# Latent layer of a four-layer trunk: a ring of three transposed tiles, value products two steps behind, another order of projections, gates directly behind their unit

## The reference

```python
proj = h @ w_in                                  # c_q 256, c_kv 128, k_rope 64, g 2048
q = (rmsnorm(c_q, q_norm_g) @ w_uq)              # 16 heads x (128 + 64)
kv = (rmsnorm(c_kv, kv_norm_g) @ w_ukv)          # 16 heads x (128 keys + 128 values)
for i in range(S // 128):                        # 8 tiles of 128 queries
    s = q_nope @ k_nope.T + q_rope @ k_rope.T    # causal: keys 0 .. 128 (i + 1)
    p = softmax(s * scale)
    outs.append(p @ v)
return (o * silu(g)) @ w_out
```

## Time and profile before

| | us |
|---|---|
| median of three runs | 2589.19 |
| the profiled execution | 2590.05 |
| its span, first to last instruction | 2588.1 |
| TensorE busy | 2365.7 (91%) |
| VectorE busy | 1569.3 (61%) |
| ScalarE busy | 1348.4 (52%) |
| GpSimd busy | 462.5 (18%) |
| granted TensorE clock, mean | 0.968 |

### The profile page before, as it was taken

The page is one execution under the profiler, slowest core; times in us unless marked ns, Lnnn a source line. Parts: engine busy times, 40 slices in busy tenths (PEclk is TensorE's granted clock), DMA queues, the critical chain, the costliest instruction groups (busy, mean ns, idle before and its releaser), DMA issues. The chain is left out here.

```text
span 2588.1 us, 43259 instructions
## 1 busy us (share of the span) xinstructions
PE 2365.7 (91%) x17364; PEld 1335.5 (52%) x17364; DVE 1569.3 (61%) x2220; ACT 1348.4 (52%) x2029; POOL 462.5 (18%) x418
## 2 busy tenths in 40 slices
PE   8999989987888888989888999999998799999987
PEld 4667654444544454445444455555454345776643
DVE  5566665765655556656546566666666465667654
ACT  4434443445545444444433677777778543444432
POOL 0000111122111102011012223233223210011011
PEclk9999999998899999999989999999999899999998
DMA  3011112214334334424331221121211121111113
GB/s 116 26 42 50 34 34 91 75 48 89 74 75 83 77 79 79 86 65 95 80 86 57 59 58 34 50 58 50 58 41 34 41 91 34 35 50 33 34 59 120
DMA packets 197721, 160.31 MB, mean 62 GB/s; under 512 B 160114, under 2 KB 161394, under 8 KB 197524
## 3 DMA queue, kind: packets, MB, share of 16 engines
q1 hardware_dynamic: 193428, 153.35, 22.4%
q0 software_dynamic: 4096, 4.20, 0.7%
HBM read 98.79 MB, written 4.19 MB: 40 GB/s over the span
## 5 line engine op out<-in xcount | busy, mean ns | idle before, releaser
L240 PE MATMUL psum<-h_hi,w_hi 128*128 128x512 f16 x1128 | 431.7, 383 | 35.7 <-ACT mla_silu_g L285 18.4
L241 PE MATMUL psum<-h_lo,w_hi 128*128 128x512 f16 x1128 | 431.5, 382 | 0.0
L242 PE MATMUL psum<-h_hi,w_lo 128*128 128x512 f16 x1128 | 431.3, 382 | 0.0
L2340 DVE SCALAR_TENSOR_TENSOR w_lo<-wf,w_hi 128x1024 f16<-128x1024 f32 (+3 forms) x194 | 231.1, 1199 | 138.8 <-ACT w_hi L2335 138.7
L256 PE MATMUL psum<-w_hi,h_hi 128*128 128x128 f16 x1504 | 256.9, 219 | 0.0
L258 PE MATMUL psum<-w_hi,h_lo 128*128 128x128 f16 x1504 | 256.5, 219 | 0.0
L257 PE MATMUL psum<-w_lo,h_hi 128*128 128x128 f16 x1504 | 256.5, 219 | 0.0
L1619 ACT ACTIVATE ssum<-psum,mla_neg_top 128x128 f32<-128x128 f32 (+7 forms) x128 | 94.7, 740 | 298.3 <-DVE mla_neg_top L1526 298.3
L1097 POOL TENSOR_TENSOR sb_al<-sb_zc,sb_ah 128x256 f16<-128x256 f32 (+2 forms) x96 | 166.2, 1732 | 373.0 <-ACT sb_ah L1062 373.0
L2335 ACT ACTIVATE w_hi<-wf 128x1024 f16<-128x1024 f32 (+3 forms) x194 | 187.0, 975 | 39.7 <-PE psum L242 19.6
L240 PEld LDWEIGHTS psum<-h_hi,w_hi 128*128 128x128 f16 x1128 | 111.3, 99 | 159.1 <-issue 42.9
(11 more groups left out here) (325 smaller groups left out, 5859.7 us busy)
## 6 DMA issues: line engine op xcount, KB each, us to landing
wf<-in_gla_out SPq DMA_DIRECT2D x32, 512.0 KB, 3.5
wf<-in_sb_in SPq DMA_DIRECT2D x32, 512.0 KB, 3.5
wf<-in_mla_out SPq DMA_DIRECT2D x20, 512.0 KB, 3.9
wf<-in_gla_v SPq DMA_DIRECT2D x16, 512.0 KB, 3.5
wf<-in_gla_g SPq DMA_DIRECT2D x16, 512.0 KB, 3.5
wf<-in_mla_gate SPq DMA_DIRECT2D x16, 512.0 KB, 3.6
wf<-in_sb_out SPq DMA_DIRECT2D x16, 512.0 KB, 3.5
xT<-in_x_T SPq DMA_DIRECT2D x16, 256.0 KB, 5.1
```

The source lines that it names most:

```text
L240: pe.matmul(out, wh[:, w], act_hi[:, k, tok], start=(i == 0), stop=False)
L241: pe.matmul(out, wh[:, w], act_lo[:, k, tok], start=False, stop=False)
L242: mm = pe.matmul(out, wl[:, w], act_hi[:, k, tok], start=False, stop=(i == last))
L2340: dve.scalar_tensor_tensor(out=self.w_lo[s % Layer.NSPLIT][:, 0:cols], in0=self.wf[s % Layer.NLOAD][:, 0:cols], scalar=W_SCALE, in1=self.w ...
```

## The change

The two transposed buffers of 4 KB each per partition become one ring of 21 blocks of 256 columns, 10.5 KB, in which the tiles of a head have fixed places, so that three tiles in a row never overlap; a transpose waits for the value product of tile t-3. In a step the value product is that of tile t-2 and stands directly behind the scores; both gaps stand behind it. From head 4 on the order of projections is `uuuuguguxxrxxr`. `weave_even` puts a `gz` that stands next in the filler directly behind its unit, in the same gap, rather than leaving it for the next one.

```diff
@@ weave_even
             out.append(filler[k])
             spent += cost(filler[k])
             k += 1
+        while 0 < k < len(filler) and filler[k][0] == "gz":
+            out.append(filler[k])
+            k += 1
     return out + filler[k:]
@@ LatentAttention.__init__
-            self.pt = [sb(f"prob_halves_T{i}", [P, 2 * T], F16) for i in range(2)]
+            self.pt = sb("prob_halves_T", [P, self.TURNED * 2 * P], F16)
-            self.kt = [t[:].bitcast(F32)[:, c * HALF:(c + 1) * HALF] for t in self.pt for c in range(2)]
+            self.kt = [self.pt[:].bitcast(F32)[:, i * HALF:(i + 1) * HALF] for i in range(4)]
@@ LatentAttention
-    ORDER = "uuuuuugrgr", "uuguuguuxrxrxx"
+    TURNED, TURNED_AT = 21, (20, 12, 15, 8, 0, 15, 8, 0)
+    ORDER = "uuuuuugrgr", "uuuuguguxxrxxr"
@@ build_items
-            main += [("s", t + 1), ("m", t + 1), ("gap", 1)] if t < last else []
-            main += [("pv", t - 1)] if t else []
+            main += [("s", t + 1), ("m", t + 1)] if t < last else []
+            main += [("pv", t - 2)] if t >= 2 else []
+            main += [("gap", 1)]
             main += [("d", t + 1)] if t < last else []
...
-        items += early + [("pv", last)] + tail
+        items += [("pv", last - 1)] + early + [("pv", last)] + tail
@@ new
+    def turned_at(self, t):
+        at = self.TURNED_AT[t % TT] * 2 * P
+        return self.pt[:, at:at + 2 * (t % TT + 1) * P]
@@ pe, item pv
-                hi, lo = (self.pt[t % 2][:, k * P:(k + 1) * P] for k in (j, i + 1 + j))
+                hi, lo = (self.turned_at(t)[:, k * P:(k + 1) * P] for k in (j, i + 1 + j))
@@ sync, item d
-            if t >= 2:
-                sp.wait_ge(self.pv_done, t - 1)
-            sp.dma_start_transpose(self.pt[t % 2][:, 0:2 * w].rearrange("p (j q) -> p j q", q=P),
+            if t >= 3:
+                sp.wait_ge(self.pv_done, t - 2)
+            sp.dma_start_transpose(self.turned_at(t).rearrange("p (j q) -> p j q", q=P),
                                    self.ph[t % 2][:, 0:2 * w]).then_inc(self.turned[t % 2], 16)
```

## The result

The changed kernel takes 2617.94 us (median of 4 runs, 2615.97 to 2621.06) against 2589.10 us of before: a ratio of 1.0117, with a 95% interval of 1.0099 to 1.0136. It is slower by 28.8 us where 25 were forecast (2615). The profiled execution took 2615.97 us with a span of 2614.0, 25.9 more than before. That is 28.1 us; the rest of the program is 2.2 us shorter.

What follows compares the result with a forecast made beforehand. VectorE and ScalarE were taken as one serial pair that bounds the kernel, not TensorE. Terms 13 (order) + 19 (clock) - 2 (gates) - 5 (end) = +25 us on 2590 gave 2615 us, range 2560 to 2640.

Steps and rivals of the forecast that it cites:

- What bounds the kernel: Latent loop: VectorE and ScalarE form one serial program; removing TensorE waits gives at most the pair's 22.6 us waiting for TensorE.
- Rival A: Whole loop: TensorE is the bound, so removing its waits gains about 45 us, to 2545 us; chance 0.10.
- B: Rival: k1 is not held, TensorE stays ahead and the pair gains, 35 us with other terms: 2555 us; chance 0.18.
- The wait at k1: Head starts, heads 4 to 14: second k unit waits for q's bank; third maximum +2.7 us even, +1.1 odd.
- R: Head start: time when q's first low half ends and k1 may start; third maximum put at R + 8.5 us.
- signs that were named: Right: heads of 52 to 56 us, maxima waiting 20 us or more. Wrong: heads under 50, third maxima under R + 7.
- Third to fifth maximum: Within a head: 16.7 us in even heads and 17.4 in odd, changes of -0.4 and -1.1 us.
- The term of 13 us: Heads 4 to 14 at full clock: new order costs +2.3 per even head, 0.0 per odd, +1.1 in head 14.
- that of 19 us: Head starts: gathered TensorE idle brings half clock, 1.7 us for each of 11 heads; bounds 0 and +35.
- Gates at once: Heads 0 to 3: gates copied out directly behind their unit, -2 us together; bounds -8 and +4.
- Last head and end: Last head, without a k unit: the 2.82 us gating wait and some lockstep go, -5 us; bounds -10 and 0.
- what the two steps behind are worth: Loop: later value products save up to 15.7 us of gating waits, only where TensorE is not late for another reason.

Runs made afterwards that it cites:

- Experiment 12: Kernel before, with the gate's table operations moved ahead of the next tile's exponential and its product behind that maximum; gates not at once: 2522.20 us.
- Experiment 5: Changed kernel, with useless matmuls filling TensorE's waits before the second q and both k units, from the fifth head on: 2602.24 us.
- experiment 9: Changed kernel with the old order of projections and the rotary additions of odd heads issued a unit earlier: 2610.89 us.
- experiment 6: Kernel before with ring and value products two steps behind, plus the rotary additions of odd heads issued a unit earlier: 2605.42 us.
- Experiment 4: Kernel before with the three-tile ring and value products two steps behind; old order, gates not at once: 2619.61 us.
- experiment 1: Changed kernel with the former order of projections, everything else as changed: 2621.03 us.
- 11: Kernel of experiment 9 with the gate's table operations and product spread as in experiment 7: 2538.15 us.
- experiment 7: Kernel before with gates at once, the gate's table operations moved ahead of the next tile's exponential and its product behind that maximum: 2522.03 us.
- experiments 2: Kernel before with the new order of projections alone: 2607.73 us.

## Why the prediction was right, and where its steps were not

**What bounds the kernel: right.** The serial pair of VectorE and ScalarE was read from one row, maxima that wait 0.9 us for TensorE, against 87% of TensorE. TensorE's waits for tiles and gates fell by about 61 us, and the loop grew. That alone does not prove it, since its idle time came back under other names (116.7 us for 100.5). Experiment 12 is the stronger proof: it took waits away between the two, aimed at none of TensorE's (its waits for gates' copies stay, 17.8 us for 18.4), and the time fell by 67 us. The 87% also overstates TensorE: by its weight loads it is busy 381.0 of 776.5 us, 49%, less than VectorE's 59%. Rival A would have needed 2545 and B 2555. (A's working is off: 67.1 us less half is 34, not 45, so 2556.)

**The wait at k1: right in place and size, incomplete in number.** R in head 7 was the end of the first low half of q, and k1 started there. The third maximum came 8.9 us after R (903.26 to 912.19) where R + 8.5 was written at full clock, or R + 10.2 with the clock's share. In even heads it came 11 us after R (963.94, R about 953.0), since k0 had already waited 2.73 us for the residual add, which I had not priced, and its clock was at half. The step from the first to the third maximum grew from 7.9 to 13.1 and 13.7 us in even heads 8 and 6, and from 9.5 to 11.1 in head 7. Of the signs that were named, the heads of 52 to 56 us did not come: even ones took 57, odd ones 50 to 51, and two of these, at 49.7 and 49.8, touch a sign of being wrong. Their mean over heads 4 to 14, 53.6, is as forecast.

**Third to fifth maximum: right in even heads (16.9 for 16.7), wrong in odd ones.** There it took 12.1 us where 17.4 stood: v1, two slabs and the second gate's product went behind the fifth maximum, and the stretch from there to the next head took 26.5 instead of 22.0. The sum of both fell by 1.9 us (-1.1 forecast), so the total did not suffer.

**The term of 13 us and that of 19 us: right in their sum, and now separable.** Heads 4 to 14 grew by 31.0 us against 32 in the two terms. Experiment 5 takes the clock away and leaves 14.6 us of these 31.0 in those heads: 16.4 for the clock (19 forecast) and 14.6 for the rest (13 forecast). The 3.2 us that head 4 lost to the filling products are still in that rest. Here the distribution is off: the even heads carry +25.0, the odd +3.2, head 14 +2.8, where 20, 8.5 and 2.8 were forecast; half clock in odd heads is partly what they had already. That 5.0 us too little and 5.3 too much cancel is luck.

The Trainium skill, "TensorE: Matmul & The Clock Gate", section "Loop structure matters more than you think", asks that matmuls stay back to back because they run cold after a long wait. The traces agree: 0.50 to 0.81 behind the waits in the changed kernel, 1.00 with them filled.

**Gates at once: the sum was small, the reason wrong.** The prediction gave it -2 us, all in heads 0 to 3. Those heads grew by 1.3 us in the changed kernel. Alone, the rule costs 4.8 us there and gains 7.6 in heads 4 to 14, where the prediction had said that it changes nothing. Beside the two steps it costs 4.9 us (experiment 9 less 6), so it may have cost, not saved, in the changed kernel.

**Last head and end: right**, -4.15 us for -5.

**The step that failed: what the two steps behind are worth.** The prediction said that their part of the change saves up to 15.7 us of gating waits and does no harm, and that the new order "decides". The gating waits fell by 8.3 us only (22.6 to 14.3), and value products began to wait 12.3 us for the gating product. Experiment 4 shows that the two steps alone cost 28.7 us, of which 12 to 14 went when the rotary additions left their place behind GpSimd's low half (experiment 6), a queue which no step of the prediction had looked at. In the changed kernel that queue does not show as a wait, since the new order moved the tile's work away from it. So the forecast hit the total because it worked out the heads as they would stand with all parts in place. Its attribution to the order alone was wrong: taking the order back gained nothing (experiment 1), and with GpSimd's place mended 8.8 us.

**What stays open.** The last 16 to 17 us of the two steps (experiment 6 against before, 11 against 7). The traces show where they go: ScalarE waits for TensorE before high halves of k and v, 15.2 us in the loop of experiment 6 and 21.3 in that of 11, where it waits 0.0 before and 1.7 in experiment 7. Why TensorE is late there they do not settle. In them the gating of the last head then stands in the third tile together with a gate, and in experiment 6 the granted clock falls at a head's start after a single idle of 3.8 us (to 0.50 from 895 to 899); which of the two it is was not tried apart. Nor was it tried why gates at once cost 4.9 us beside the two steps and gain 4.9 without them.

## What to carry to other kernels

- Ask which engine's waits for the busiest engine are near zero. If a serial pair of others hardly waits for it, its own waits are slack: 61 us of them were removed, came back elsewhere, and nothing was gained, while removing 52 us of waits between the pair gave 67. Count the waits of both engines of the pair, at every kind of instruction: the maxima alone hid the cost in experiments 2 and 4.
- When a value is consumed one step later, list everything behind it in every queue, that of a nearly idle engine too. And compute the reuse distance of rotating buffers anew after each reordering: four units in a row on three banks waited for the first one's readers in each of these heads.
- Undoing one part of a change measures that part only where the parts do not share a wait. Here the parts alone sum to +42 and the whole is +30, and undoing the part that was thought to decide gave nothing back, since another wait took its place.

## What the runs showed of the hardware

Useless matmuls in TensorE's waits made the kernel 15.7 us faster: the granted clock at head starts went from between 0.50 and 0.81 to 1.00, and the work behind the waits ran at 2.4 GHz. Around the idles of 2.73 and 2.41 us that end at 949.91 and 953.13, with three matmuls between them, it was 1.00 from 944 to 948, 0.83 from 948 to 952 and 0.50 from 952 to 956. A single idle of 2.78 us in experiment 4 was followed by 0.57 in the next 4 us, one of 1.17 us at the same place in experiment 6 by 1.00. Over the loops, the clock is 0.93 with 116.7 us of idle for TensorE (the changed kernel), 0.96 with 100.5 (before) and 0.98 with 59.8 (experiment 7).
